# Two adds per head of a depthwise convolution, done on GpSimd instead of VectorE, in a two-layer hybrid attention and convolution trunk

## What is computed

```python
proj = h @ w_mix_in[l]
q, k, v, u, gates = jnp.split(proj, [...], axis=-1)
o = diff_attention(q, k, v, lam, rel_bias)              # 8 heads, two softmax maps each
y_attn = (rms_norm(o, subln_gain[l]) * (1 - lam_init)).reshape(B, S, ATTN_W) @ w_attn_branch[l]

a, g = jnp.split(u, 2, axis=-1)
z = a * jax.nn.sigmoid(g)
z = causal_depthwise_conv(z, w_dw, width=31) + b_dw
y_conv = jax.nn.silu(layer_norm(z, ln_g, ln_b)) @ w_out
merged = sigmoid(ga) * y_attn + sigmoid(gb) * y_conv
x = x + g2 * (merged @ w_mix_out[l])
```

## Time and profile before

| what | value |
|---|---|
| median of 3 runs | 2756.42 us (2755.35 to 2757.57) |
| the profiled execution | 2755.38 us, span 2753.7 us |
| mean granted TensorE clock | 0.978 |
| busy: TensorE, VectorE, ScalarE, GpSimd | 94%, 63%, 39%, 3% |
| one head of the mixing loop | about 44.46 us |

### The profile page before, as it was taken

One profiled execution on the slowest core, in us unless ns is written; L12 is line 12 of the kernel. 1 busy time (PEld: TensorE's weight loads), 2 busy tenths in 40 slices (PEclk: granted clock), 3 DMA queues, 4 the chain that ended last, 5 costly groups with the idle time before them and its releaser, 6 DMA issues.

```text
span 2753.7 us, 35127 instructions
## 1 busy us (share of the span) xinstructions
PE 2585.2 (94%) x11186; PEld 2030.9 (74%) x11186; DVE 1748.2 (63%) x2545; ACT 1060.4 (39%) x1497; POOL 81.7 (3%) x162
## 2 busy tenths in 40 slices
PE   4899998999999989999979999989999999899997
PEld 2688886776767767888858888867766678688886
DVE  3655567799998555543345556669999965655433
ACT  2433322444443434343234342244444443443422
POOL 0000010000000000000000001100000000000000
PEclk9999998999999999999989999989999999999998
DMA  5444474222222233433324446622222223343332
GB/s 221 142 149 142 151 224 142 81 76 72 80 80 84 84 114 115 152 122 95 97 83 145 153 129 208 211 66 79 76 73 83 77 87 122 101 143 107 97 92 93
DMA packets 472262, 320.39 MB, mean 116 GB/s; under 512 B 11303, under 2 KB 447785, under 8 KB 471176
## 3 DMA queue, kind: packets, MB, share of 16 engines
q1 hardware_dynamic: 445260, 227.69, 28.1%
q0 software_dynamic: 21888, 83.90, 8.9%
q10 hardware_dynamic: 5052, 8.02, 1.0%
HBM read 314.52 MB, written 5.05 MB: 116 GB/s over the span
## 4 chain that ended last, share of the span: by engine, by line
PE 68%; DVE 16%; issue 11%; ACT 3%; ACTq 1%; DVEq 1%
PE bank L1045 21%; PE bank L1047 21%; PE bank L1046 21%; DVE conv_part L858 5%; DVE rstd L616 3%; DVE w_lo L605 2%; ACTq L420 1%; ACT w_hi L377 1%; DVE probs L890 1%; PE bank L1063 1%; PE bank L1064 1%; PE bank L1065 1%; PE bank L1100 1%; DVE probs L906 1%; PE bank L1127 1%
## 5 line engine op out<-in xcount | busy, mean ns | idle before, releaser
L605 DVE TENSOR_TENSOR w_lo<-w_raw,w_hi 128x1024 fp32r<-128x1024 f32 (+1 forms) x434 | 522.6, 1205 | 721.5 <-ACT w_hi L377 720.6
L1046 PE MATMUL bank<-h_lo,w_hi 128*128 128x512 f32 x2336 | 911.3, 390 | 0.0
L1045 PE MATMUL bank<-h_hi,w_hi 128*128 128x512 f32 x2208 | 885.9, 401 | 17.9 <-DVE w_lo L605 17.8
L1047 PE MATMUL bank<-h_hi,w_lo 128*128 128x512 f32 x2208 | 862.9, 391 | 0.0
L377 ACT ACTIVATE w_hi<-w_raw 128x1024 fp32r<-128x1024 f32 (+1 forms) x434 | 452.4, 1043 | 912.8 <-PE bank L1047 893.1
L1045 PEld LDWEIGHTS bank<-h_hi,w_hi 128*128 128x128 f32 x2208 | 415.5, 188 | 134.9 <-issue 52.2
L1046 PEld LDWEIGHTS bank<-h_lo,w_hi 128*128 128x128 f32 x2336 | 440.1, 188 | 89.9 <-issue 3.8
L1047 PEld LDWEIGHTS bank<-h_hi,w_lo 128*128 128x128 f32 x2208 | 415.4, 188 | 89.0
L858 DVE SCALAR_TENSOR_TENSOR conv_part<-glu,conv_taps,conv_part 128x512 f32<-128x512 f32 x464 | 316.6, 747 | 0.0
L1045 PE MATMUL bank<-s_hi,w_hi 128*128 128x512 f32 x704 | 274.9, 390 | 0.0
L1047 PE MATMUL bank<-s_hi,w_lo 128*128 128x512 f32 x704 | 274.0, 389 | 0.0
(11 more groups left out here) (158 smaller groups left out, 2296.5 us busy)
## 6 DMA issues: line engine op xcount, KB each, us to landing
w_raw<-in_ffn_w_in SPq DMA_DIRECT2D x176, 512.0 KB, 3.8
ada_raw<-in_ada_w POOLq DMA_DIRECT2D x144, 512.0 KB, 4.7
w_raw<-in_w_mix_in SPq DMA_DIRECT2D x112, 512.0 KB, 3.7
w_raw<-in_ffn_w_out SPq DMA_DIRECT2D x64, 512.0 KB, 3.6
w_raw<-in_ffn_w_out SPq DMA_DIRECT2D x32, 384.0 KB, 3.1
w_raw<-in_w_mix_out SPq DMA_DIRECT2D x18, 512.0 KB, 3.6
ada_first<-in_ada_w POOLq DMA_DIRECT2D x8, 1024.0 KB, 24.4
w_raw<-in_w_attn_branch SPq DMA_DIRECT2D x16, 512.0 KB, 3.6
```

The lines of the kernel that those rows point to most:

```text
L605: dve.tensor_tensor(wlo[slot][:, 0:n, :], raw[slot][:, 0:n, :], whi[slot][:, 0:n, :].bitcast(F32), ALU.subtract).then_inc(w_lo[slot], 1)
L1045: pe.matmul(acc, wh, hi[:, k0 + k, :], start=first and k == 0, stop=False)
L1046: pe.matmul(acc, wh, lo[:, k0 + k, :], start=False, stop=False)
L1047: mm = pe.matmul(acc, wl, hi[:, k0 + k, :], start=False, stop=last and k == n - 1)
```

## The change

The two adds of `chains` leave VectorE's stream, and GpSimd gets a loop over the heads of a layer that does them, placed between its loads for the first feed-forward part and those for the second. `chains` keeps only its wait for the taps. Ahead of each add GpSimd does a small add on one column of `spare`; the tile `spare` gets a second column for that, and VectorE's small memset in `scores` moves to it.

```diff
-    spare = at("spare", [P, 1], F32)
+    spare = at("spare", [P, 2], F32)
...
+        def carry_wait():
+
+            pool.tensor_tensor(spare[:, 0:1], eps[:, 0:1], eps[:, 0:1], ALU.add)
+
+        def conv_sum(l, h):
+
+            q = h + l * HEADS
+            c = tile(C2, h)
+            pool.wait_ge(sem("csum"), q)
+            pool.wait_ge(sem("tap_done"), (q + 1) * DVE_TAPS)
+            carry_wait()
+            pool.tensor_tensor(c, CAB[0][:, :], CAB[1][:, :], ALU.add).then_inc(sem("c_ready"), 1)
+            pool.wait_ge(sem("ssum_clear"), l * ZEROS + 1 + ZERO_CONV)
+            pool.wait_ge(sem("c_ready"), q + 1)
+            carry_wait()
+            pool.tensor_tensor(SSUM[:, :], SSUM[:, :], c, ALU.add).then_inc(sem("csum"), 1)
...
             with pool.Fori(0, CHUNKS_OUT) as g:
                 ada_chunk(l, g + (2 + CHUNKS_IN[0]), l * NMOD + CHUNK_SEQ["ffn1_out"] + g)
+            with pool.Fori(0, HEADS) as h:
+                conv_sum(l, h)
+
...
                     dve.wait_ge(sem("tap_done"), (q + 1) * DVE_TAPS)
-                    dve.tensor_tensor(tile(C2, h), CAB[0][:, :], CAB[1][:, :], ALU.add).then_inc(sem("c_ready"), 1)
-                    dve.wait_ge(sem("csum"), q)
-                    dve.wait_ge(sem("ssum_clear"), l * ZEROS + 1 + ZERO_CONV)
-                    dve.wait_ge(sem("c_ready"), q + 1)
-                    dve.tensor_tensor(SSUM[:, :], SSUM[:, :], tile(C2, h), ALU.add).then_inc(sem("csum"), 1)
...
-                        dve.memset(spare[:, 0:1], 0.0)
+                        dve.memset(spare[:, 1:2], 0.0)
```

## The result

The changed kernel takes 2771.86 us (median of 5 runs, 2769.68 to 2773.97) against 2756.42 before (5 runs); the ratio is 1.0055, 95% interval 1.004 to 1.0069. It is slower by 15.4 us.

What follows compares the result with a forecast made beforehand. VectorE was taken to pace the loop over heads, TensorE following with 2.0 us to spare. 2755.4 + 5.4 (loop, blocked) + 9.6 (end of the convolution) = 2770.4 us, range 2739 to 2781.

Steps and rivals of the forecast that it cites:

- The bound: Loop over heads in the mixing stage: VectorE, 96% busy, sets the pace; TensorE has 2.0 us to spare per head.
- blocked: Likeliest case, chance 0.38: VectorE's two-input operations stand while a GpSimd add runs; 2770.4 us.
- free: Rival, free overlap: VectorE doesn't feel GpSimd's adds in the loop; 2741.2 us, chance 0.30.
- the reason given: After the last tap: two-tensor reading is at VectorE's limit, so GpSimd's two further streams are not free.
- The sum: Blocked sum, loop: beside 2.6 us of adds VectorE does only L901, L903 and its idle time, about 0.75 us.
- The loop's term: Loop over heads: VectorE stands 1.85 us where it worked 1.40, +0.45 us per head, 12 x 0.45 = +5.4 us.
- the 4.60 us wait: Last head: VectorE waits 4.60 us at w_lo for ScalarE, swallowing any gain just before; so six heads count, not seven.
- The end's term: End of the convolution: sum 3.5 us later plus 1.3 for the clock, 4.8 per layer, +9.6 us in both.
- the low clock: After TensorE's idle of over 5 us at the convolution's end, its lower clock adds 1.3 us per layer.
- The add's length: GpSimd's 512-column add: 1.2 us, plus 0.1 per small add, 1.3 together, between 0.95 and 1.7.
- the order that I had assumed: Convolution's end: VectorE does both w_lo first, to about 866.8, then GpSimd's 2.6 us of adds, ending at 869.5.
- kept out: Rival: VectorE's two-input chain leaves GpSimd no opening until it stops; loop 0, end 9.6, 2765.0 us, chance 0.15.

Runs made afterwards that it cites:

- run 6: Against the kernel before: both adds of heads 0 to 6 on GpSimd beside VectorE's 3.35 us reciprocal, last taps to two own tiles; 2740.72 us, ratio 0.9945.
- run 8: Kernel before, all adds kept on VectorE, plus two GpSimd adds per head (0 to 6) on an own tile, nobody waiting; 2772.68 us, ratio 1.0061.
- run 5: Against the kernel before: only the second add of heads 0 to 6 on GpSimd, held back until VectorE's 3.35 us reciprocal; 2746.75 us, ratio 0.9965.
- run 7: Against the kernel before: first add on VectorE, second replaced by GpSimd clearing the running sum, nothing read; 2748.33 us, ratio 0.9972.
- run 9: Kernel before, all adds on VectorE, plus per head (0 to 6) one small GpSimd add and a 1024-column clearing; 2760.07 us, ratio 1.0020.
- run 12: Kernel before plus two GpSimd adds per head (0 to 6) on an own tile, released after the tenth tap; 2755.53 us, ratio 1.0001.
- run 3: Against the kernel before: only the first add (accumulators into the tile) on GpSimd, all heads, running sum on VectorE; 2758.80 us, ratio 1.0016.
- run 4: Against the kernel before: only the second add (tile into the running sum) on GpSimd, all heads; 2761.28 us, ratio 1.0021.
- run 2: Against the kernel before: only the last head's two adds of each layer on GpSimd; 2767.32 us, ratio 1.0037.
- run 1: Against the kernel before: adds of heads 0 to 6 on GpSimd, the last head's two on VectorE; 2761.19 us, ratio 1.0020.

## Why the prediction was right, point by point

**The bound** was read rightly: VectorE paces the loop. Shortening it by 1.21 us per head shortened the run by 14.8 us (run 6; 12 x 1.21 = 14.5), and TensorE still waits 1.1 us then.

**The decision between blocked and free** fell as forecast, and mainly for the reason given: L906 of before ends 0.08 us behind the first add, L944 0.55 us behind the second, run 8 charges the time where nobody waits for GpSimd, and runs 5 and 6 take it away by moving the adds beside an operation with one input. One step was not argued. The reason given covers operations with two tensors, and 0.72 of the 1.63 us that VectorE stands fall on L906, which has one input at the doubled rate. The sum had it only because it listed nothing but L901 and L903 as running on. The rule of the Trainium skill, "SBUF — State Buffer", section "Who interferes with whom", fits: two-tensor operations against GpSimd reads (1.60 us for 0.69), not against writes (run 7), doubled-rate ones against writes as well (run 9). Which of two waiting engines comes next is another matter: having waited longer gave GpSimd no turn in run 12.

**The loop's term** was +0.45 us per head and measured +0.42, from two terms that were each some 0.2 too large. VectorE stood 0.72 + 0.91 = 1.63 us, not 1.85; and the removal was worth 1.21 us, not 1.40 (run 6). I had also counted six heads. There were seven: I said that whatever is gained just before the 4.60 us wait goes into it. That holds for a gain, but the block also delays `combine(0)` itself, on which TensorE's next turning of weights waits (the new 0.8 us), and so ScalarE and that wait's end. The seventh costs 0.38. The runs bear this out: where L906 ends 0.72 us later, the seventh head is 0.35 longer (run 3), where 0.48 later, 0.14 (run 8), where 0.37 later, 0.04 (run 9), and nothing where only the first tap is held (run 4). So 5.4 forecast, 5.8 measured.

**The end's term** was 3.5 + 1.3 us per layer and measured 3.3 + 1.2 in the first. I had GpSimd wait for both `w_lo`; in fact the turns alternated, and the first add got in between the two. The second `w_lo` needs ScalarE's rounded part, which came at 868.13, 0.3 us before the first ended. That it came late isn't needed for an opening: in run 4 it was there at 865.95, 0.8 us before the first `w_lo` ended, and GpSimd's small add got in all the same. Why there is an opening between two `w_lo` and none in a row of taps (run 12), and why in run 4 it served the small add alone, stays open. The sum came out near mine because the second add then had to let the second `w_lo` pass. In the second layer the low clock lasted longer and cost 2.4 us, not 1.3; in runs 2 and 4 it cost 1.4 to 2.3.

**The add's length**: 1.28 and 1.34 us where I took 1.2; a small add 0.2, not 0.1.

**Luck.** The direction and the mechanism were forecast. That the total comes within 1.5 us of 2770.4 is in part luck: two errors of 0.2 us per head cancel, the alternation at the end costs about as much as the order that I had assumed, and the missing seventh head and the longer low clock add only 0.4 and 1 us.

**The rival "kept out"** was wrong for this change: GpSimd gets in right after `w_lo`, where L901 with its two columns follows. But what it describes does happen, in run 12.

## What to carry to other kernels

An operation moved off a busy VectorE to GpSimd is only gone if what VectorE does meanwhile leaves GpSimd its turn. Look at the kind of the VectorE operations in that stretch: here one with two tensor inputs in SBUF (1.60 us for 0.69), or one with a single input at doubled rate (1.01 for 0.29), stood still for the rest of a GpSimd add. Release GpSimd's work at the start of a long operation with one input at plain rate (here a reciprocal), or in an unbroken row of two-tensor operations, which here held it off by itself until that point, and give it slack of a whole iteration; keep on VectorE the last one of a series, for which somebody waits at once. In this kernel the two adds of the same fourteen heads cost 0.20% at one place (run 1) and gave 0.55% at another (run 6).

## What was not expected

- A GpSimd operation on one column can take 5.74 us when it has to wait for its turn; unhindered it takes 0.2. So a GpSimd row of this profile can be mostly waiting.
- In an unbroken row VectorE lost nothing at all to GpSimd (44.46 us per head, run 12); with small steps that wait for each other the same adds cost it 1.32 (run 8). In the changed kernel GpSimd's second pair got in within the half microsecond from 606.47 to 606.97 that holds one short operation and two waits.
- GpSimd's add of a tile to itself takes 1.03 us where nothing hinders it, of two tiles 1.25 to 1.34.
- After the same idle of TensorE the clock came out differently: behind the next stop of the second layer the first matmul was at full clock before and at the lower level after, with idles of 3.18 and 3.12 us:

```profile
2235.68 0.47 PE L1045 MATMUL bank<-ao_hi,w_hi 128*128 128x512 f32 x1 [3.18 <-DVE gate_a L960]
```

```profile
2251.30 0.77 PE L1060 MATMUL bank<-ao_hi,w_hi 128*128 128x512 f32 x1 [3.12 <-DVE gate_a L975]
```

The first is of the kernel before, the second of the changed one. From the layer norm's reciprocal to the next long one, which takes in this stop, it is 132.75 us in the first and 133.94 in the second. But that isn't the change's doing: the same stretch, in either layer, takes 131.1 to 133.9 us in the other traces, and 131.1, 132.7 and 133.9 all occur in runs 8 and 12, which leave the end of the convolution as it was. So 1.2 of the 16.9 us between the two profiled spans are chance, and what decides it stays open.
